# Level products of a blockwise triangular inversion, moved from the full array to its two diagonal quarters

## The reference, cut to what matters

```python
m = beta[..., :, None] * jnp.einsum('bhnid,bhnjd->bhnij', k, k) * dec_strict
sol = lax.linalg.triangular_solve(m + jnp.eye(C, dtype=m.dtype), rhs,
                                  left_side=True, lower=True, unit_diagonal=True)
u_bar, w = sol[..., :DV], sol[..., DV:]
```

## Time and profile before

| | us |
|---|---|
| median of 3 runs | 2622.28 (2621.74 to 2623.23) |
| the profiled execution | 2621.7 |
| its span | 2619.9 |
| PE busy, PE weight loads busy | 2499.7, 2396.5 |
| DVE, POOL, ACT busy | 1036.3, 808.8, 675.5 |
| mean granted clock of PE | 0.976 of full speed |

### The profile page before, as it was taken

How to read it: one execution, slowest core, us unless ns; L and a number is a source line. 1 busy time by engine, 2 the same in 40 slices (tenths; PEclk the granted TensorE clock), 3 DMA queues, 4 the chain that set the end, 5 groups by cost and what they waited for, 6 DMA issues and landing times. The chain is left out here.

```text
span 2619.9 us, 40153 instructions
## 1 busy us (share of the span) xinstructions
PE 2499.7 (95%) x15943; PEld 2396.5 (91%) x15943; DVE 1036.3 (40%) x1603; ACT 675.5 (26%) x1350; POOL 808.8 (31%) x711
## 2 busy tenths in 40 slices
PE   5899999999999998998999999999999979997998
PEld 4799999999988898998999999999999879997886
DVE  6510011222455654002555555455555443323332
ACT  7111111111145431111232223222332243212222
POOL 1111121111111111114465456454555214332222
PEclk9899999999999999998999999999999879999999
DMA  5112412100111121242223324443224355543343
GB/s 159 47 66 107 193 63 74 66 33 33 66 50 49 49 74 68 74 136 68 82 76 111 111 81 127 159 122 97 81 78 108 119 174 179 198 162 140 114 145 106
DMA packets 200143, 264.95 MB, mean 101 GB/s; under 512 B 16176, under 2 KB 175296, under 8 KB 194432
## 3 DMA queue, kind: packets, MB, share of 16 engines
q1 hardware_dynamic: 200064, 263.86, 31.2%
HBM read 164.54 MB, written 99.29 MB: 101 GB/s over the span
## 5 line engine op out<-in xcount | busy, mean ns | idle before, releaser
L178 POOL TENSOR_TENSOR w_hi<-w_raw,zero 128x1024 fp32r<-128x1024 f32 x77 | 146.9, 1908 | 1243.0 <-PE dense L426 943.3
L424 PE MATMUL dense<-h_hi_first,w_hi 128*128 128x352 f32 x1080 | 355.2, 329 | 15.5 <-ACT row_y L671 8.4
L425 PE MATMUL dense<-h_lo_first,w_hi 128*128 128x352 f32 x1080 | 352.2, 326 | 0.0
L426 PE MATMUL dense<-h_hi_first,w_lo 128*128 128x352 f32 x1080 | 351.7, 326 | 0.0
L425 PE MATMUL dense<-h_lo_second,w_hi 128*128 128x352 f32 x1080 | 349.8, 324 | 0.0
L426 PE MATMUL dense<-h_hi_second,w_lo 128*128 128x352 f32 x1080 | 348.7, 323 | 0.0
L424 PE MATMUL dense<-h_hi_second,w_hi 128*128 128x352 f32 x1080 | 347.7, 322 | 0.0
L1314 PE MATMUL gate_bank<-h_hi_first,w_hi 128*128 128x352 f32 x768 | 274.4, 357 | 5.1 <-SPq L1232 4.4
L1314 PE MATMUL gate_bank<-h_hi_first,w_lo 128*128 128x352 f32 x768 | 249.5, 325 | 0.0
L1314 PE MATMUL gate_bank<-h_lo_first,w_hi 128*128 128x352 f32 x768 | 249.3, 325 | 0.0
L424 PEld LDWEIGHTS dense<-h_hi_first,w_hi 128*128 128x128 f32 x1080 | 206.1, 191 | 19.9 <-ACT row_y L671 8.7
(11 more groups left out here) (212 smaller groups left out, 4625.4 us busy)
## 6 DMA issues: line engine op xcount, KB each, us to landing
w_raw<-in_w_in SPq DMA_DIRECT2D x77, 512.0 KB, 5.8
rows_then_inputs<-scratch_feat SPq DMA_DIRECT2D x16, 1856.0 KB, 9.2
scratch_feat<-row_y SPq DMA_DIRECT2D x28, 1056.0 KB, 4.9
gate<-scratch_gates SPq DMA_DIRECT2D x12, 2112.0 KB, 8.7
scratch_gates<-gate_row SPq DMA_DIRECT2D x96, 176.0 KB, 1.9
o_raw<-scratch_branch_out SPq DMA_DIRECT2D x6, 2112.0 KB, 12.9
scratch_merged<-merged SPq DMA_DIRECT2D x48, 176.0 KB, 1.8
rows_then_inputs<-in_x_prompt SPq DMA_DIRECT2D x16, 512.0 KB, 3.7
```

Of the source, the lines that this page charges most:

```text
L178: nc.gpsimd.tensor_tensor(self.hi[:, p], raw, zeros, ALU.add).then_inc(self.high_ready, 1)
L424: nc.tensor.matmul(out, w_hi[:, p, k], h_hi[:, k, cols], start=(k == 0), stop=False)
L425: nc.tensor.matmul(out, w_hi[:, p, k], h_lo[:, k, cols], start=False, stop=False)
L426: mm = nc.tensor.matmul(out, w_lo[:, p, k], h_hi[:, k, cols], start=False, stop=(k == KD - 1))
```

## The change

In levels with 2s < n, which are levels 1 to 5 of a full chunk, the matrices have no entries outside two diagonal blocks of 64 x 64. Each of the two products is therefore formed in two calls a head, one with rows 0 to 63 and one with rows 64 to 127, each with the 64 weight columns of the same range and with 32 moving columns. They write partitions 0 to 63 and 64 to 127 of the bank. The first call of a group (head 0, rows 0 to 63) keeps all 128 weight columns, so that it writes all 128 partitions. DVE's two operations of the level are also split in two, one for each half of the partitions. Level 6 and the sample chunk keep one call a head. Semaphores count as before, on the last call.

```diff
+                        parts = [slice(a, a + min(n, HALF)) for a in range(0, n, HALF)] if 2 * s < n else [slice(0, n)]
+
+                        def packed(rows):
+                            return slice(rows.start // 2, rows.stop // 2)
                         for h in range(HEADS):
-                            mm = matmul(halves_packed(z_bank[0:n, h:h + 1, 0:n // 2], s)[:, 0], M[0:n, h, 0:n],
-                                        second_halves(XT[0:n, h:h + 1, 0:n], s)[:, 0], start=True, stop=True)
+                            for rows in parts:
+
+                                out = rows if h or rows.start else slice(0, n)
+                                mm = matmul(halves_packed(z_bank[out, h:h + 1, packed(rows)], s)[:, 0], M[rows, h, out],
+                                            second_halves(XT[rows, h:h + 1, rows], s)[:, 0], start=True, stop=True)
                         mm.then_inc(z_ready, 1)
...
                         for h in range(HEADS):
-                            mm = matmul(halves_packed(xt_bank[0:n, h:h + 1, 0:n // 2], s)[:, 0], X[0:n, h, 0:n],
-                                        halves_packed(Z[0:n, h:h + 1, 0:n // 2], s)[:, 0], start=True, stop=True)
+                            for rows in parts:
+                                out = rows if h or rows.start else slice(0, n)
+                                mm = matmul(halves_packed(xt_bank[out, h:h + 1, packed(rows)], s)[:, 0], X[rows, h, out],
+                                            halves_packed(Z[rows, h:h + 1, packed(rows)], s)[:, 0], start=True, stop=True)
                         mm.then_inc(xt_products, 1)
...
                         dve.wait_ge(z_ready, c * (LEVELS - 1) + l)
-                        level = level_masks[0:n, l:l + 1, 0:n // 2].to_broadcast([n, HEADS, n // 2])
-                        tt(halves_packed(Z[0:n, :, 0:n // 2], s), halves_packed(z_bank[0:n, :, 0:n // 2], s),
-                           halves_packed(level, s), ALU.mult).then_inc(z_taken, 1)
+
+                        size = min(n, HALF) if 2 * s < n else n
+                        for a in range(0, n, size):
+                            rows, cols = slice(a, a + size), slice(a // 2, (a + size) // 2)
+                            level = level_masks[rows, l:l + 1, cols].to_broadcast([size, HEADS, size // 2])
+                            last = tt(halves_packed(Z[rows, :, cols], s), halves_packed(z_bank[rows, :, cols], s),
+                                      halves_packed(level, s), ALU.mult)
+                        last.then_inc(z_taken, 1)
...
-                        new = second_halves(XT[0:n, :, 0:n], s)
-                        tt(new, new, halves_packed(xt_bank[0:n, :, 0:n // 2], s),
-                           ALU.subtract).then_inc(xt_updated, 1)
+                        for a in range(0, n, size):
+                            rows, cols = slice(a, a + size), slice(a // 2, (a + size) // 2)
+                            new = second_halves(XT[rows, :, rows], s)
+                            last = tt(new, new, halves_packed(xt_bank[rows, :, cols], s), ALU.subtract)
+                        last.then_inc(xt_updated, 1)
```

## The result

The changed kernel takes 2671.88 us (median of 4 runs, 2670.55 to 2673.51), the kernel before, on the same chip, 2622.01 (2620.98 to 2623.23): a ratio of 1.019, 95% interval [1.0173, 1.0208], **+50 us**. The forecast was 2692 with a range of 2626 to 2718. The direction came true, and so did the mechanism of its largest term, the changes of form. The order that it gave the best chance, quarters one after another, did not: they run side by side. Two terms were off in opposite directions, and level 6, the length of PE's program and the clock, for which its sum had nothing, cost time.

What follows compares the result with a forecast made beforehand. The prediction took PE, busy 95%, to bound the kernel. From 2621.7 us it added 160 groups at 0.46 us (74 us), less 3 us absorbed, giving 2692 us, with a range of 2626 to 2718.

Steps and rivals of the forecast that it cites:

- quarters one after another: Main case for PE's groups in levels 1 to 5: quarters do not overlap, switches cost; 2692 us, 2678 to 2717, chance 0.50.
- side by side: Rival for PE's groups: two quarters work in parallel, switches still cost; 2625 to 2652 us, middle 2645, chance 0.27.
- The phase is bound by PE: Chunk phase: PE is the limit, so a change in its instruction string goes almost one to one into time, 16 times.
- Price of a quarter product: PE's groups, levels 1 to 5: 0.06 us a quarter record, 1.05 us a group instead of 0.86, +0.19 us.
- The first rival: PE's groups: two quarters work in parallel at 0.03 us a record, switches stay; middle 2645 us, chance 0.27.
- Price of a change of form: PE's groups: each change of the array's shape costs 0.09 us, three a group, +0.27 us.
- Sum per group: PE's groups, levels 1 to 5: 0.19 + 0.27 = 0.46 us more each, 74 us over 160 groups.
- Absorbed in waits: PE's existing waits for ACT's copy of X and for Z in level 6 hide 3 to 5 us; 3 subtracted.
- DVE's edits at nothing: DVE's split operations, at most +0.14 us each, are covered by PE's work and cost nothing; without cover 22 us.
- The clock falls: Rival: levels of the full chunks drop to half clock for a tenth of their time; +37 us, 2730 or more, chance 0.05.
- the sign: Full chunks: a chunk period near 57 us instead of 52.67 would show the forecast right.
- The second rival: PE's groups: quarters in parallel and switches hidden, deciding if a switch costs under 0.077 us; 2585 us, chance 0.10.

Runs made afterwards that it cites:

- e2: The changed kernel with every quarter product 64 x 64, head 0's too, and a semaphore instruction ahead of each group: 2612.15 us, 0.9968 of the kernel before.
- e8: The changed kernel with only head 3's product of each group in two 64 x 64 quarters, heads 0 to 2 on the full array: 2654.66 us, 1.0131 of the kernel before.
- e1: The kernel before with only DVE's two operations of levels 1 to 5 split in halves and Z zeroed once: 2631.48 us, ratio 1.0043.
- e6: The kernel before with 288 more semaphore instructions in PE's loop body, one ahead of each gate product: 2642.15 us, ratio 1.0083.
- e4: The changed kernel with DVE's gate differences moved earlier, portions of 2, 2, 2, 1 behind levels 2 to 5: 2693.24 us, 1.027 of the kernel before.
- e3: The changed kernel with each group issuing all four heads' upper quarters first, then the lower ones: 2694.33 us, 1.0279 of the kernel before.

## Why the prediction came out as it did

- **The phase is bound by PE, so its string counts one to one.** Right: 26 of 52 us are the groups themselves, and e2 shows it in the other direction.
- **Price of a quarter product, 0.06 and one after another, +0.19 us a group.** Wrong: 0.03, and the group's records take 0.24 less than before (2 x 0.109 + 14 x 0.029 = 0.62). The first rival's mechanism is what happened; it had a chance of 0.27 against 0.50. The row that 0.06 came from the earlier trace rows has a single quarter in the array and could not speak for two. The sentence of the Trainium skill that tiles work in parallel ("TensorEngine Tiling (Array Packing)", Key Properties), quoted at that rival, was right.
- **Price of a change of form, 0.09, three times: +0.27.** The mechanism right, the size wrong: with records at 0.62, three seams are 0.44 in the changed kernel, 0.145 each, and 0.13 each in e2 and e8. The first seam of a group taken alone, 0.25 less 0.16, is the 0.09 of the earlier trace rows; the other two are dearer (0.17 each) than any row at full clock showed.
- **Sum per group +0.46.** Measured +0.20 (0.24 saved, 0.44 paid): 160 x 0.195 is 31 us instead of 74, from two errors, 0.43 too dear and 0.17 too cheap.
- **Absorbed in waits, 3 to 5 us.** Right in size: 31 less the 26.2 found (24.8 and 1.4) is 5, at ACT's copy of X in levels 3 and 5. At Z in level 6 nothing was absorbed; that wait grew from 0.19 to 0.91.
- **DVE's edits at nothing.** Wrong in level 6, right in levels 1 to 5, which e1 leaves as they were. The forecast saw DVE arriving 0.14 later there and set longer seams in front against it. But DVE's run from XT to Z starts only when level 5's last product is done, so seams in front delay both ends and hide nothing. Then the operation L1696 doubled beside POOL. Together 10 us (e1: 10.5).
- **No row on the length of PE's program.** The forecast counted the added instructions and their time, not their room. 8 us, shown by e6 and by e8's absence of it.
- **The clock falls.** Not in the levels of the steady chunks, which stood at 1.00. It stayed low longer in chunk 0, for 3 us of time; and it had a large share in e4's loss.
- **The total** came out inside the range and 20 under the forecast by luck, through errors that cancel: records 160 x 0.43 = 69 too dear and 2 too little absorbed, against seams 160 x 0.17 = 27 too cheap, 10 for level 6, 8 for the pauses, 3 for the clock, 4 at the two ends. Neither story that the range was made of gives it with its own prices: quarters one after another asked for 2678 to 2717, side by side for 2625 to 2652. A chunk takes 55.1 us (even ones), not the 57 named as the sign.
- **The second rival** (2585, faster) asked for a seam under 0.077; at 0.145 it was far off. It took one form less per group to be faster than before: e2, with two seams of 0.13.

Open: +2.6 us before the first chunk (1224.5 to 1228.2 in the kernels of the study, with no order that fits the edits) and +1.5 behind the last.

## What to carry to other kernels

Products that fill only diagonal quarters of the array are worth packing when neighbours in the order alternate between quarters and every record of a group has the same form; count the changes of form first, since here one costs as much as 4 to 5 quarter records, and a single full-width product inside the group decided between faster and slower. An engine at 40% can still set a wait: find the one stage where it is nearly late, and look at what its operations will lie beside once they move. And count the instructions that a change adds to a loop body, beside their time.

## What the hardware showed

- Records of fp32 quarter products in opposite corners of the array start in pairs 6 to 7 ns apart, a pair every 58 ns; full ones every 107 ns. By the two series of e3, later ones of the free quarter start ahead of waiting ones of the other.
- A change between full and quarter form costs 0.13 us at full clock (e2, e8). What it consists of no run here separates.
- A PE loop body of 1670 or 1750 instructions was not fetched again in each pass (55 or 56 packets), one of about 1885 was (111). Then PE paused 1.5 to 3.3 us at each jump back (more behind chunk 7, where it waits 3.4 us anyway), and the granted clock fell to 0.50 for 3 to 4 us behind the pauses of e6.
- A 0.28 us VectorE operation beside a 2.48 us GpSimd one took 2.43 us. A 0.41 us one took 0.41 where it started 2 to 7 ns ahead of a GpSimd addition, and 0.95 where it started 0.19 to 0.20 us behind one.
